# RWKV-7 chunk inversion in 32x32 blocks, and the chunk recurrence spread over four quarters of TensorE's array

## The reference

```python
def step(S, inp):
    r_t, w_t, k_t, v_t, a_t, b_t = inp
    sa = jnp.einsum('bhij,bhj->bhi', S, a_t)
    S = (S * w_t[:, :, None, :] + sa[..., None] * b_t[:, :, None, :]
         + v_t[..., None] * k_t[:, :, None, :])
    y_t = jnp.einsum('bhij,bhj->bhi', S, r_t)
    return S, y_t
...
y = _layer_norm(y, lnx_g.reshape(A_HEADS, A_HEAD_DIM), lnx_b.reshape(A_HEADS, A_HEAD_DIM), GN_EPS)
y = y + jnp.sum(r * k * r_k.astype(jnp.float32), axis=-1, keepdims=True) * v
y = y.reshape(bsz, t, c).astype(x.dtype) * g
return y @ w_o
```

## Time and profile before

| | |
|---|---|
| three runs | 1299.5, 1300.0, 1301.41 us; median 1300.0 us |
| profiled execution | 1299.6 us, first to last instruction; 0.4 us under the median |
| PE busy | 1269.2 us, 98% of the span |
| DVE, ACT, POOL busy | 894.2, 679.4, 83.8 us |
| chain that ended last | PE 83%, DVE 9%, ACT 6% |
| inversion on PE | from 712.19 to about 751.9 us |
| recurrence on PE | from 752.25 to 781.87 us, where the output projection starts |
| PE busy in 752 to 782 us | 28.88 of 30 us |
| granted clock in both | 1.00, the higher of the two levels (2.4 GHz) |

### The profile page before, as it was taken

How to read it: one execution, slowest core, us unless ns; L and a number is a source line. 1 busy time by engine, 2 the same in 40 slices (tenths; PEclk the granted TensorE clock), 3 DMA queues, 4 the chain that set the end, 5 groups by cost and what they waited for, 6 DMA issues and landing times.

```text
span 1299.6 us, 23670 instructions
## 1 busy us (share of the span) xinstructions
PE 1269.2 (98%) x10054; PEld 1098.1 (84%) x10059; DVE 894.2 (69%) x1467; ACT 679.4 (52%) x1228; POOL 83.8 (6%) x103
## 2 busy tenths in 40 slices
PE   9999999999999999999999999999999999999997
PEld 6978888889967888888898997888897987788886
DVE  6886666674685666656898848666668366766666
ACT  6874444463584454544663434444455477445452
POOL 3000500000060000000001600000000000000000
PEclk9999999999999999999999999999999999999999
DMA  9445454544412555553443003654555441455550
GB/s 351 159 184 200 184 190 184 188 188 166 165 62 81 200 195 194 194 195 130 164 161 131 5 36 114 219 193 188 195 194 194 176 161 61 187 194 194 195 194 33
DMA packets 17496, 214.45 MB, mean 165 GB/s; under 512 B 1960, under 2 KB 2128, under 8 KB 4720
## 3 DMA queue, kind: packets, MB, share of 16 engines
q1 hardware_dynamic: 15888, 205.43, 41.9%
q0 software_dynamic: 1504, 7.52, 1.6%
HBM read 211.87 MB, written 1.06 MB: 164 GB/s over the span
## 4 chain that ended last, share of the span: by engine, by line
PE 83%; DVE 9%; ACT 6%; issue 1%; DMA 1%; SPq 0%; DVEq 0%; ACTq 0%
PE psum L696 25%; PE psum L670 14%; PE psum L676 7%; PE psum L486 4%; PE psum L487 4%; PE psum L488 4%; DVE w_low L1996 3%; ACT w_high L1443 2%; PE psum L1054 2%; PE psum L1198 1%; PE psum L585 1%; PE psum L1245 1%; PE psum L1373 1%; PE psum L581 1%; PE psum L577 1%; PE psum L1069 1%
## 5 line engine op out<-in xcount | busy, mean ns | idle before, releaser
L1996 DVE TENSOR_TENSOR w_low<-ring,w_high 128x1024 fp32r<-128x1024 f32 x372 | 443.4, 1227 | 188.5 <-ACT w_high L1443 188.5
L1443 ACT ACTIVATE w_high<-ring 128x1024 fp32r<-128x1024 f32 x372 | 372.7, 1048 | 139.7 <-PE psum L696 105.4
L696 PE MATMUL psum<-w_high,up_split 128*128 128x512 f32 x1024 | 287.6, 391 | 0.8 <-DVE up_split L2151 0.8
L696 PEld LDWEIGHTS psum<-w_high,up_split 128*128 128x128 f32 x1024 | 190.3, 188 | 40.5 <-issue 2.7
L670 PE MATMUL psum<-act_split,w_high 128*128 128x512 f32 x768 | 191.6, 391 | 0.0
L696 PE MATMUL psum<-w_low,up_split 128*128 128x512 f32 x512 | 163.2, 390 | 0.0
L670 PEld LDWEIGHTS psum<-act_split,w_high 128*128 128x128 f32 x768 | 139.6, 189 | 26.0
L1544 ACT ACTIVATE up_split<-work 128x256 fp32r<-128x256 f32 x112 | 46.8, 418 | 159.4 <-DVE work L2144 148.8
L486 PE MATMUL psum<-act_split,w_high 128*128 128x256 f32 x448 | 129.1, 288 | 0.3 <-DVE act_split L2162 0.3
L487 PE MATMUL psum<-act_split,w_high 128*128 128x256 f32 x448 | 126.7, 283 | 0.0
L488 PE MATMUL psum<-act_split,w_low 128*128 128x256 f32 x448 | 126.7, 283 | 0.0
(11 more groups left out here) (360 smaller groups left out, 1873.7 us busy)
## 6 DMA issues: line engine op xcount, KB each, us to landing
ring<-weights SPq DMA_DIRECT2D x95, 2048.0 KB, 7.5
work<-rows POOLq DMA_DIRECT2D x4, 1024.0 KB, 5.1
ring<-weights SPq DMA_DIRECT2D x4, 512.0 KB, 8.4
work<-rows POOLq DMA_DIRECT2D x4, 512.0 KB, 5.4
x<-x_in SPq DMA_DIRECT2D x2, 512.0 KB, 4.7
work<-t_bias POOLq DMA_DIRECT2D x1, 1024.0 KB, 8.4
out<-x SPq DMA_DIRECT2D x4, 256.0 KB, 2.1
con<-consts SPq DMA_DIRECT2D x1, 576.0 KB, 22.0
```

The costliest lines, as they stand in the source:

```text
L696: last = mm(bank(acc[(th, n)]), up_split[:, m, a, P * th:P * th + P], w[:, f], start=start and i == 0, stop=stop and i == len(pairs) - 1, ...
L1443: A(high[:, HIGH_SLOT[name], f], ring[:, n % RING, f], ACT.Copy).then_inc(weights_high, 1)
L1996: V.tensor_tensor(low[:, n % RING, f], ring[:, n % RING, f], high[:, HIGH_SLOT[name], f].bitcast(f32), ALU.subtract).then_inc(weights_spli ...
```

## The change

In the inversion every 64x64 matrix is handled as two diagonal 32x32 blocks and one corner. The blocks are packed (`inv_m`): the upper left block on a unit's first 32 partitions, the lower right on its last 32. All buffers of the inversion are half as large. Levels 1 to 4 work on four 32x32 tiles of the array, one for each quarter of the partitions. Level 5 is of another kind: `corner_product` and `corners` compute the corner and move the upper left block's column to its place, ACT copies that to the right half of `y_wide`, and DVE writes its left half (`inv_wide`). POOL's masks stop at level 4.

Outside it the half of a head's tokens is set by feature chunk, `at_half(hf, c)`. `turned` therefore drops its transposes and uses `centred`'s plain matmuls with the identity; a result that used one bank uses a pair, odd chunks in the second (`pair`, `odd_even`); `g` and `u` share a pair. In the recurrence, steps between tokens and head features (`g` from the state, both parts of the state, `turn_heads`) alternate quarters from chunk to chunk. `y` stays in one bank, and its part from the state moves behind `u`, in two runs with waits on PE's own `y_even` and `y_odd` between them; `y`'s part from the values moves behind `g`'s part from the state.

```diff
 for _t in range(NT):
     _turns(("wkv_g", _t), 1, 0)
-    _turns(("wkv_u", _t), 1, 1)
+    _turns(("wkv_u", _t), 1, 0)
     if _t:
-        _turns(("wkv_turned", _t - 1), 1, 2)
+        _turns(("wkv_turned", _t - 1), 1, 6)
     if _t < NT - 1:
-        _turns(("wkv_s", _t), 1, 3)
-    _turns(("wkv_y", _t), 1, 4 + _t)
+        _turns(("wkv_s", _t), 1, 2)
+    _turns(("wkv_y", _t), 1, 4 + _t % 2)
...
-            def centred(name, src):
+            def turned(name, src, through="diag"):
...
+                                c, tc = 2 * ((4 * i + j) // NT) + (upper ^ hf), (4 * i + j) % NT
+                                t = (c * NT + tc) * CH
                                 last = mm(psum[half(upper), BANK[q + hf], j * CH:j * CH + CH],
-                                          work[half(hf), src, t:t + CH], cst("center")[half(hf), :], start=True, stop=True)
+                                          work[half(hf), src, t:t + CH], cst(through)[half(hf), :], start=True, stop=True)
...
+            def masked_product(q, i):
+                open_bank(q)
+                for n in range(8):
+                    for b in range(4):
+                        last = mm(psum[block(b), BANK[q], QB * n:QB * n + QB], inv_lm[block(b), 8 * i + n, :],
+                                  inv_x[block(b), 8 * i + n, :], start=True, stop=True)
+                last.then_inc(bank_filled, 1)
+            def merged(q, l, i):
...
+                for n in range(8):
+                    for b in range(4):
+                        cols = inv_y[block(b), 8 * i + n, :].rearrange("p (b a s) -> p b a s", a=2, s=s)[:, :, 1, :]
+                        got = psum[block(b), BANK[q], 16 * n:16 * n + 16].rearrange("p (b s) -> p b s", s=s)
+                        last = mm(got, inv_t[block(b), 8 * i + n, :], cols, start=True, stop=True)
...
+            def corner_product(q, i):
...
+                    for b in (0, 2):
+                        last = mm(psum[block(b + 1), BANK[q], QB * n:QB * n + QB], gb_u[block(b), 8 * i + n, 0, QB:CH],
+                                  inv_x[block(b), 8 * i + n, :], start=True, stop=True)
...
+            def corners(q, i):
...
+                    for b in (0, 2):
+                        y = inv_y[block(b + 1), 8 * i + n, :]
+                        mm(got[block(b), :], inv_t[block(b + 1), 8 * i + n, :], y, start=True, stop=True)
+                        last = mm(got[block(b + 1), :], cst("eye")[block(b + 1), :], y, start=True, stop=True)
...
-            for l in range(1, LEVELS):
+            for l in range(1, LEVELS - 1):
...
+            l = LEVELS - 1
+            for i in range(4):
+                pe.wait_ge(sig("inv_turned"), 4 * (l - 1) + i + 1)
+                corner_product(TURN[("inv_t", l)] + i, i)
+            for i in range(4):
+                read_out(pe, TURN[("inv_t", l)] + i)
+                corners(TURN[("inv_xy", l)] + i, i)
...
-                f = slice(512 * i, 512 * i + 512)
-                done(V.transpose(buf(RW_X)[:, f], buf(RW_Y)[:, f]), "inv_turned")
+                f = slice(256 * i, 256 * i + 256)
+                done(V.transpose(buf(RW_X)[:, f], buf(RW_LM)[:, 1024:2048][:, f]), "inv_turned")
...
-                    taken(V.tensor_tensor(cols, cols, bank(q, 256).rearrange("p (b s) -> p b s", s=s), ALU.add), q)
-                    if l < LEVELS - 1:
-                        settle()
-                        turn_blocks(i)
+                    taken(V.tensor_tensor(cols, cols, bank(q, 128).rearrange("p (b s) -> p b s", s=s), ALU.add), q)
+                    settle()
+                    turn_blocks(i)
```

## The result

The changed kernel takes 1340.7 us (1336.2 to 1342.2, four runs) where the kernel before takes 1300.0 on the same chip, a ratio of 1.0303 (95% interval 1.0287 to 1.032). The forecast was 1282.8 us with a range of 1279.5 to 1290.0, so both the sign and the size are wrong. The profiled execution took 1336.2 us, 1334.3 of it the span.

The account below looks back on a forecast made before the run. The prediction took PE's records to bound the inversion, with DVE next. Gains of 16.0 us there and 1.7 in the recurrence, less 0.45 ahead, made 17.25 off 1300.0: 1282.8 us, range 1279.5 to 1290.

Parts of the forecast that it names:

- The inversion, PE alone: Inversion: 8 ns per record in four 32x32 tiles, so PE's work takes 20.5 us for some 39.7.
- the slower rival: Inversion: each record costs a fixed 29 to 30 ns whatever its tile; kernel 1331 us; chance 0.07.
- inversion with DVE: Inversion: DVE becomes the limit at 2.7 us a level; the stage takes 24 us for 40.06, gain 16.0 us.
- What bounds the kernel now: Inversion: paid by PE's 1,280 records at 29 to 30 ns, with DVE the next limit, not far below.
- The clock: Inversion: clock falls throughout, 16 ns per record, no gain there, kernel 1299 us; chance 0.05.
- DVE: Inversion: smaller adds and transposes take 0.67 us a group for 1.09, 2.7 us for four groups.
- the 2.4 us of idle behind level 1: Inversion: PE idles from 8.5 to 10.9 us after the first product, until DVE's first transpose of level 2.
- Ahead of it: Before the inversion: plain matmuls for transposes in `turned` delay PE by `bt` and the first `kt` pair; loss 0.45 us.
- The recurrence: Recurrence: steps in four quarters take 0.5 us for 0.93; gain 1.7 us, bounds 0 and 2.5.

Follow-up runs that it names:

- e3: The changed kernel with operands of inversion levels 1 to 4 cut to their upper 16 bits, one record per matmul instead of two: 1312.4 us, ratio 1.0086.
- e4: The kernel before plus 384 tiny matmuls, 128 long ones and 512 tiny ones on zeros ahead of the inversion: 1340.2 us in a single run.
- e8: The kernel before with the products of its old inversion spread over four 64x64 quarters, same number of records: 1303.7 us, ratio 1.0023.
- e2: The changed kernel with the old inversion on 64x64 units, the rest of the change kept: 1307.3 us, ratio 1.0044.
- e6: The changed kernel with two 128x512 matmuls of zeros ahead of each group of the new inversion: 1344.6 us, ratio 1.0346.
- e1: The kernel before with the new inversion alone; layout, transposes and recurrence as before: 1337.4 us, ratio 1.0279.
- e5: The kernel before with 16 tiny matmuls ahead of each of the old inversion's 40 groups, 640 records more: 1320.6 us, ratio 1.0165.

## Why the prediction was wrong

**The inversion, PE alone: this step failed.** I took "8 ns per record" from a burst of 32 records, bounded it from bursts of 24 to 128, and multiplied it by 2,432. The 8 ns are right for a burst (8.7 ns at full clock in the first), but no burst in the earlier trace rows is longer than one packet, so none could show a sustained rate. In the changed kernel's inversion a record costs 28.6 ns (69.6 us / 2,432), over the break-even of 16.8 that the slower rival named. The forecast's term for PE alone was 20.5 us, its inversion with DVE 24; the packets take 19 x 3.66 = 69.6 us. The trace of before held the means to see it: the packets of q8, one per 128 records, every 4.0 us in the stage that changes.

**The rivals.** The slower one gave 1331 us with 0.07; that it came near the size is luck, for its mechanism is another. It laid 29 ns on the array for each record, and e3 and e4 show 8 to 9 ns there. The Trainium skill's floor of 25 ns from matmul to matmul (TensorE: Matmul & The Clock Gate, "Back-to-back issue gap"), which I set aside, is close to the pace of long runs here (27 to 29 ns) and far from that inside a burst (8 ns): taken as a sustained rate it would have given the right sign. I weighed it only against bursts. No run here shows that the floor and the pace of the packets have one cause. The Trainium skill also describes the instruction memory as refilled in blocks of 16 KB, with their fetch mostly hidden (Runtime: NRT & Kernel Launch, "Instruction fetch mechanics"). The block size agrees with the 16 KB packets here; that the fetch is mostly hidden does not, with pauses of 1.5 to 2.1 us between the bursts of the changed kernel's inversion.

**What bounds the kernel now.** "The inversion is paid by PE's records" held by count, but not as array time alone: e8 took a third of the products' time away and gained nothing. In the earlier trace rows 29 and 30 ns stand for 32 and 64 columns, and I read this as a price of the tile. e8 bears that out, since a merge still takes (2.46 - 0.22) / 77 = 29 ns inside a burst behind a pause. What I missed is the second limit beside it: 128 records of 29 to 30 ns are 3.7 to 3.9 us, about what a packet takes.

**The clock.** It did fall, for nearly the whole inversion, against 0.05, but the 1299 us of that rival did not follow. Of the sum it is a small part: the spacing is 3.40 us ahead of the fall and 3.42 behind it. It costs directly where TensorE has work in store, at the start of the recurrence: (1 - 0.50) x 3.7 + (1 - 0.81) x 4 = 2.6 us at most.

**DVE.** Its operations shrank as forecast, to 0.29 us for the add and 0.45 for the transpose:

```profile
724.90 0.29 DVE L2637 TENSOR_TENSOR work<-work,psum 128x128 f32<-128x128 f32 x1 [1.77 <-PE psum L1209]
725.23 0.45 DVE L2611 STREAM_TRANSPOSE work<-work 128x256 f32<-128x256 f32 x1
725.79 0.29 DVE L2637 TENSOR_TENSOR work<-work,psum 128x128 f32<-128x128 f32 x1
```

They stand 0.89 us apart for 0.67; a group of 64 records takes as long (64 x 13.6 ns = 0.87), so their own pace was not seen. DVE waited for TensorE all through; the 2.4 us of idle behind level 1 did not arise.

**Ahead of it** was mis-sized: 2.5 us lost for 0.45. In the changed kernel `turned` and the Gram products have pauses by issue of 1.23, 1.22 and 0.56 us, which the forecast had at nothing. **The recurrence** was wrong in sign: 2.5 us lost for 1.7 gained. Its two pauses (1.25 + 0.74) and the low clock at its start (up to 2.6) come to 4.6 us, so the quartered steps themselves may have gained 2. e2 gives about the same (2.3 us lost, with 2.5 of pauses and up to 1.7 by the clock), but no run tests that split by itself.

## What to carry to other kernels

Count a stage's instructions as well as its array time. With fp32 matmuls (two records each) a stage of small tiles needs at least 3.4 to 4 us per 128 records here, so making a record cheaper than about 27 to 31 ns gains nothing in a long run, and splitting work into more and smaller matmuls costs in proportion. Take the price of a record from runs longer than two packets, and look for idle time by issue at a constant count of records; more columns per matmul, or long matmuls between short ones, should then be worth more than a fuller array; no run here tried that as an improvement.

## What the runs showed of the hardware that was not expected

- TensorE's instructions came in 16 KB packets of 128 records, 3.4 to 4.3 us apart where TensorE waited for them; after a long slow stretch (17 us) one whole packet beyond the current one was in store. The spacing is the sum of three parts: 1.0 to 1.9 us from a burst's start to the start of q8's next packet, 0.9 to 1.5 us for the packet, and 1.2 to 1.6 us from its end to the next burst (once 1.9, in e6). Where the spacing is longer (up to 4.0 us in the changed kernel, 4.3 in e3, 4.2 in e8), it is mostly by the first two. In the changed kernel it takes three values, near 3.4, 3.7 and 4.0 us. Why it varies is open.
- In e1's unchanged recurrence, at 29 ns per record, TensorE paused 2.79 us by issue. The packet that ended that pause started at 809.52 us, 7.3 us after the one before it; between 804 and 814 us another queue, q0, moved 1.05 MB. Whether it held the packet up is not shown.
- Where only bursts and pauses stood, the granted clock fell to 0.50 within one or two of them, and it fell as well in e5, from 1.00 to 0.75 behind 4 us in which TensorE was busy throughout, with tiny records among the others. That 640 of them cost up to 10.6 us by the clock and 12 by themselves was in none of my sums.
